# One MoE layer on one core: the shared expert as a group of its own, and one more place for weight tiles

## The reference, cut to what matters

```python
scores = sigmoid(t @ router_w)                    # 64 experts, 8 chosen for each token
gate   = normalised scores of the chosen 8 * 2.5
routed = sum over experts e of (silu(t @ w_gate[e]) * (t @ w_up[e]) * gate[:, e]) @ w_down[e]
shared = (silu(t @ ws_gate) * (t @ ws_up)) @ ws_down
out    = x + g2 * (routed + shared)
```

## Time and profile before

| | us |
|---|---|
| median of 3 runs | 643.5 (642.98 to 643.97) |
| the profiled execution | 645.71 |
| its span, first to last instruction | 643.9 |

### The profile page before, as it was taken

The page is one execution under the profiler, slowest core; times in us unless marked ns, Lnnn a source line. Parts: engine busy times, 40 slices in busy tenths (PEclk is TensorE's granted clock), DMA queues, the critical chain, the costliest instruction groups (busy, mean ns, idle before and its releaser), DMA issues.

```text
span 643.9 us, 11140 instructions
## 1 busy us (share of the span) xinstructions
PE 581.9 (90%) x4568; PEld 406.1 (63%) x4568; DVE 209.9 (33%) x474; ACT 168.2 (26%) x309; POOL 33.6 (5%) x79
## 2 busy tenths in 40 slices
PE   0789999999999999989999999596999999998685
PEld 0478777688877575756675757363567666675352
DVE  0297867787822222111212222020121212121103
ACT  3164727572622121111121212010212121212111
POOL 1240210011100000000000000000000000000002
PEclk9989999999999999999999999898999999999889
DMA  8999599989988999999999999999999999999994
GB/s 329 387 344 389 211 364 383 411 312 397 420 348 365 396 423 415 422 419 421 421 420 420 420 421 419 421 422 421 420 420 421 421 421 421 421 419 420 421 386 155
DMA packets 50662, 252.55 MB, mean 392 GB/s; under 512 B 5912, under 2 KB 11680, under 8 KB 26288
## 3 DMA queue, kind: packets, MB, share of 16 engines
q1 hardware_dynamic: 48240, 246.37, 94.4%
q0 software_dynamic: 1840, 4.21, 2.0%
q10 hardware_dynamic: 528, 1.21, 0.5%
HBM read 250.06 MB, written 1.72 MB: 391 GB/s over the span
## 4 chain that ended last, share of the span: by engine, by line
PE 66%; DMA 19%; SPq 6%; ACT 4%; DVE 2%; issue 1%; POOL 0%; POOLq 0%; DVEq 0%; ACTq 0%
PE bank L1278 21%; PE bank L1354 12%; DMA ring<-in_w_up 8%; PE bank L1249 6%; PE bank L1295 6%; DMA ring<-in_w_down 6%; SPq L556 4%; PE bank L848 3%; DMA ring<-in_w_mod 2%; SPq L627 2%; PE bank L890 2%; PE bank L898 2%; PE bank L894 2%; DMA ccol<-in_c 2%; DMA ring<-in_w_in 1%; PE bank L1011 1%
## 5 line engine op out<-in xcount | busy, mean ns | idle before, releaser
L1278 PE MATMUL bank<-ring,xe 128*64 128x256 f32 (+1 forms) x1520 | 176.1, 397 | 10.7 <-DMA ring<-in_w_up 9.0
L1278 PEld LDWEIGHTS bank<-ring,xe 128*64 128x64 f32 (+1 forms) x1520 | 110.8, 131 | 49.7 <-issue 23.7
L1354 PE MATMUL bank<-ring,actT 128*64 128x512 f32 (+1 forms) x384 | 85.5, 615 | 4.8 <-DMA ring<-in_w_down 3.2
L2325 DVE TENSOR_TENSOR act_e<-bank,sil 128x256 f32<-128x256 f32 x26 | 11.0, 425 | 190.1 <-ACT sil L1741 190.1
L1754 ACT ACTIVATE yhi<-bank,gslot 128x512 fp32r<-128x512 f32 x50 | 34.4, 688 | 113.2 <-PE bank L1354 113.2
L2339 DVE SCALAR_TENSOR_TENSOR ylo<-bank,gslot,yhi 128x512 fp32r<-128x512 f32 x50 | 37.5, 750 | 80.7 <-ACT yhi L1754 80.7
L1741 ACT ACTIVATE sil<-bank 128x256 f32<-128x256 f32 x26 | 10.0, 385 | 194.2 <-PE bank L1278 194.2
L1249 PE MATMUL bank<-pone,hhi 128*128 128x256 f32 x200 | 50.6, 291 | 0.0
L1249 PE MATMUL bank<-pone,hlo 128*128 128x256 f32 x200 | 49.6, 285 | 0.0
L1354 PEld LDWEIGHTS bank<-ring,actT 128*64 128x64 f32 (+1 forms) x384 | 25.2, 130 | 34.9 <-issue 34.7
L1278 PE MATMUL bank<-rows_tile,xe 128*64 128x256 f32 (+1 forms) x128 | 33.5, 422 | 11.1 <-DMA ring<-in_w_up 6.3
(11 more groups left out here) (382 smaller groups left out, 847.5 us busy)
## 6 DMA issues: line engine op xcount, KB each, us to landing
ring<-in_w_gate SPq DMA_DIRECT2D x49, 1024.0 KB, 25.6
ring<-in_w_down SPq DMA_DIRECT2D x48, 1024.0 KB, 26.3
ring<-in_w_up SPq DMA_DIRECT2D x46, 1024.0 KB, 26.4
ring<-in_w_mod SPq DMA_DIRECT2D x12, 2048.0 KB, 13.8
ring<-in_w_in SPq DMA_DIRECT2D x5, 2048.0 KB, 15.7
gb<-in_w_up SPq DMA_DIRECT2D x5, 1024.0 KB, 24.9
spare<-in_w_gate SPq DMA_DIRECT2D x4, 1024.0 KB, 26.9
ring<-in_w_out SPq DMA_DIRECT2D x2, 2048.0 KB, 18.8
```

The lines of the kernel that those rows point to most:

```text
L1278: ins = mm(bank[6][j * w:(j + 1) * w, part * FE:(part + 1) * FE], xe[:, k, slots], weights[:, k, :], start=(k == 0), stop=(k == KD - 1))
L1354: ins = mm(bank[4 + h][j * w:(j + 1) * w, :], actT[:, f, j * w:(j + 1) * w], weights[:, f, 512 * h:512 * h + 512], start=(f == 0), stop=(f ...
```

## The change

The tokens of the shared expert are no longer read from `hT`. Group 7 (`SHARED`) is followed by one more gather, group 8, of all 256 tokens: `pone` is filled with a full one-hot pattern (`every_token`), and `xe` then holds all tokens in transposed form. The shared gate and up products read `xe`. Both are now made in one place, in group 7 behind the second step's `activations_turned`; then the gather of the next routed group follows, and `shared_down`. The numbers of all later gathers go up by one. `sg0` and the half product in group 2 are gone. `ws_gate` and `ws_up` are read in the layout `(p k) f`, whose rows are 8 KB long. The memory of `hT` becomes a place for tiles, `OVER_HT`: tile 16 is loaded there once `hb1_1` is made, and each later tile replaces the one used 17 before it.

```diff
-STEPS, GROUPS = 6 + 10 * TURNS, 3 + 5 * TURNS
+STEPS, GROUPS = 6 + 10 * TURNS, 4 + 5 * TURNS
+SHARED = 5 * (TURNS - 1) + 2
-FILL = [0, 1, OVER_Y, 2, 3, 4, 5, 6, 7, 8, 9, 10, OVER_XN, SPARE, OVER_GB, 11]
+FILL = [0, 1, OVER_Y, 2, 3, 4, 5, 6, 7, 8, 9, 10, OVER_XN, SPARE, OVER_GB, 11, OVER_HT]
-        plan += banks("sg0:4 pos:1 counts:5")
+        plan += banks("pos:1 counts:5")
...
-            sp.dma_start(ws[:, 0:EW].rearrange("p (k f) -> p k f", k=KD),
-                         t["ws_gate"][0].rearrange("(k p) f -> p k f", k=KD)).then_inc(wsg_loaded, 16)
+            sp.dma_start(ws[:, 0:EW], t["ws_gate"][0].rearrange("(p k) f -> p (k f)", k=KD)).then_inc(ws_loaded, 16)
...
+            product(sp, "hb1_1")
+            load_first(NTILE + 4)
...
-                        ins = mm(ps[:, j * 256:(j + 1) * 256], w[:, k, j::JF], hT[:, k, :], start=(k == 0), stop=(k == KD - 1))
+                        ins = mm(ps[:, j * 256:(j + 1) * 256], w[:, k, j::JF], xe[:, k, :], start=(k == 0), stop=(k == KD - 1))
-            pe.wait_ge(wsg_loaded, 16)
-            complete("sg0", shared_product(claim("sg0"), 0, (0,)))
+            def shared_gate_up(group):
+                pe.wait_ge(x_copied, group * 4 + 4)
+                pe.wait_ge(ws_loaded, 48)
+                shared_product(bank[7], 0).then_inc(sg_filled, 1)
+                shared_product(bank[4], EW).then_inc(su_filled, 1)
...
-                if shared == "gate":
-                    shared_gate()
-                elif shared == "rest":
-                    shared_up()
                 gate_up(kind, 1, n + 1, unit, group, again, spread=ends)
...
-                if not last:
+                if shared:
+                    for q in range(4):
+                        gather(q, group + 1)
+                elif not last:
                     gather(0, group + 1)
                 activations_turned(n + 1)
+                if shared:
+                    shared_gate_up(group + 1)
+                    pe.wait_ge(sg_copied, 1)
+                    gather(0, group + 2)
+                    pe.wait_ge(sact_ready, 1)
...
                     for q in range(1, 4):
-                        gather(q, group + 1)
-                if shared == "rest":
+                        gather(q, next_group(group))
+                if shared:
                     shared_down()
...
                 if par == 1 and not last:
                     gathered(group + 1)
+                if shared:
+                    shared_gate()
+                    gathered(group + 2)
...
+                    if shared:
+                        dve.wait_ge(x_filled, (SHARED + 1) * 4 + 4)
+                        one_hots(following, e + 2 * kind, posm_s)
+                        shared_act()
                     turned(following, 0, n_pair + 1)
```

More of the change, by code:

```diff
@@ L66 @@
 FIRST_STEP = [sum(1 if v in QUAD_UNITS else 2 for v in range(u)) for u in range(UNITS)]
-SPARE, OVER_GB, OVER_XN, OVER_Y, OVER_ROWS = NTILE, NTILE + 1, NTILE + 2, NTILE + 3, NTILE + 4
-FILL = [0, 1, OVER_Y, 2, 3, 4, 5, 6, 7, 8, 9, 10, OVER_XN, SPARE, OVER_GB, 11]
+SPARE, OVER_GB, OVER_XN, OVER_Y, OVER_ROWS, OVER_HT = (NTILE + i for i in range(6))
+FILL = [0, 1, OVER_Y, 2, 3, 4, 5, 6, 7, 8, 9, 10, OVER_XN, SPARE, OVER_GB, 11, OVER_HT]
 ROWS_FREE = len(FILL) + 4
@@ L368, in build @@
         out_done = sem("out_done")
-        tile_loaded = [sem(f"tile_loaded{i}") for i in range(NTILE + 5)]
+        tile_loaded = [sem(f"tile_loaded{i}") for i in range(NTILE + 6)]
         last_columns = [sem(f"last_columns{i}") for i in range(2)]
@@ L1161, in _, with shared_product @@
             turn_back(1)
-            def shared_product(ps, off, parts=range(JF)):
+            def shared_product(ps, off):
                 w = ws[:, off:off + EW].rearrange("p (k f) -> p k f", k=KD)
-                for j in parts:
+                for j in range(JF):
                     for k in range(KD):
-                        ins = mm(ps[:, j * 256:(j + 1) * 256], w[:, k, j::JF], hT[:, k, :], start=(k == 0), stop=(k == KD - 1))
+                        ins = mm(ps[:, j * 256:(j + 1) * 256], w[:, k, j::JF], xe[:, k, :], start=(k == 0), stop=(k == KD - 1))
                 return ins
-            pe.wait_ge(wsg_loaded, 16)
-            complete("sg0", shared_product(claim("sg0"), 0, (0,)))
             pe.wait_ge(chosen_ready, 1)
@@ L1222, in gather_first @@
                 evacuated(pe, "x2T3")
-                evacuated(pe, "sg0")
+                evacuated(pe, "rt0")
                 pe.wait_ge(first_stream, 1)
@@ L1237, in gather_first, with next_group @@
                             ins.then_inc(x_filled, 1)
+            def next_group(group):
+                return group + (2 if isinstance(group, int) and group == SHARED else 1)
             def gather(q, group):
@@ L1347, in down @@
                         if par == 1 and not last:
-                            pe.wait_ge(x_copied, group * 4 + 7)
+                            pe.wait_ge(x_copied, next_group(group) * 4 + 3)
                     elif par == 0:
@@ L1380, in sort_slots, with two_steps @@
                 ins.then_inc(sorted_filled, 1)
-            def two_steps(kind, e, n, group, unit, following, gates=gate_s, before=True, starts=False, shared=None, ends=False,
+            def two_steps(kind, e, n, group, unit, following, gates=gate_s, before=True, starts=False, shared=False, ends=False,
                           again=False):
@@ L1438, in first_round @@
                 for it in range(TURNS):
-                    two_steps(QUAD, 24 * it + 8, 10 * it + 4, 5 * it + 2, 6 * it + 2, PAIR, shared=("gate", "rest")[it])
+                    group = 5 * it + 2
+                    two_steps(QUAD, 24 * it + 8, 10 * it + 4, group, 6 * it + 2, PAIR, shared=(group == SHARED))
                     for i in range(4):
-                        two_steps(PAIR, 24 * it + 16 + 4 * i, 10 * it + 6 + 2 * i, 5 * it + 3 + i, 6 * it + 4 + i,
+                        two_steps(PAIR, 24 * it + 16 + 4 * i, 10 * it + 6 + 2 * i, next_group(group) + i, 6 * it + 4 + i,
                                   PAIR if i < 3 else QUAD)
@@ L1719, in _ @@
             A(table_load[:, :], rstd[:, 1, 0:1], ACT.Silu)
-            ps = product(act, "sg0")
-            drain("sg0", A(ssil[:, 0, :], ps[:, 0:NST * P], ACT.Silu))
             def gathered_first():
@@ L1737, in gathered, with pair @@
                       ACT.Copy).then_inc(x_copied, 1)
-            def pair(par, n_pair, group, last=False, starts=False, ends=False, more=0):
+            def pair(par, n_pair, group, last=False, starts=False, shared=False, ends=False, more=0):
                 act.wait_ge(e_filled, n_pair + 1)
@@ L1758, in shared_gate @@
                 act.wait_ge(sg_filled, 1)
-                A(ssil[:, 1, :], bank[7][:, NST * P:2 * NST * P], ACT.Silu).then_inc(sg_copied, 1)
+                A(ssil[:, :, :].rearrange("p a b -> p (a b)"), bank[7][:, :], ACT.Silu).then_inc(sg_copied, 1)
             def keep_g2(n, first):
@@ L1773, in two_steps @@
                     keep_g2(0, NST)
-                pair(1, n + 1, group, last, ends=ends, more=more)
+                pair(1, n + 1, group, last, shared=shared, ends=ends, more=more)
             def first_round():
@@ L1779, in first_round @@
                 two_steps(2, 1)
-                two_steps(4, 2, shared=True)
-                with act.Fori(3, GROUPS - 1) as it:
+                with act.Fori(2, SHARED) as it:
                     two_steps(it * 2, it)
+                two_steps(SHARED * 2, SHARED, shared=True)
+                with act.Fori(SHARED + 1, GROUPS - 2) as it:
+                    two_steps(it * 2, it + 1)
                 two_steps(STEPS - 2, GROUPS - 1, last=True, ends=True)
@@ L2320, in turned, with pair @@
                 ins.then_inc(t_copied, 1)
-            def pair(kind, par, e, n_pair, following, starts=False, ends=False, more=0):
+            def pair(kind, par, e, n_pair, following, starts=False, shared=False, ends=False, more=0):
                 dve.wait_ge(e_silu, n_pair + 1)
@@ L2343, in pair @@
                         sorted_out()
-                    one_hots(following, e + 2 * kind, posm_s)
+                    if shared:
+                        every_token()
+                    else:
+                        one_hots(following, e + 2 * kind, posm_s)
             def finish_all(par, n_pair):
@@ L2362, in two_steps, with every_token @@
             def two_steps(kind, e, n, following, starts=False, shared=False, ends=False, more=0):
[L2363 to L2366, removed]
+                pair(kind, 0, e, n, following, starts, shared, more=more)
+                pair(kind, 1, e, n + 1, following, shared=shared, ends=ends, more=more)
+            def every_token():
+                for s in range(NST):
+                    ins = V.tensor_scalar(pone[:, s, :, :].rearrange("p a b -> p (a b)"), iota[:, :], gate[:, s, 0:1, 1], None,
+                                          ALU.is_equal)
```

(5 more changed lines are left out.)

19 lines of the change are left out of this document (4 added, 15 removed).

## The result

The changed kernel took 645.64 us (median of 7, 644.53 to 646.49), the kernel before 643.38 (7 runs): a ratio of 1.0035, 95% interval 1.002 to 1.005. A second set, of an unchanged copy, gave 1.0043 (1.0028 to 1.0059). The change makes the kernel slower by 2.3 us. The forecast was 643.9 us, no change, with a range up to 646.7 and 0.38 on slower. The time lies in the range, but not where the forecast put it. Single executions of one kernel spread more than the 0.15% given ahead of the forecast: 28 of the kernel before lie between 641.65 and 644.85 us, 0.5% apart. Only medians of many show a difference of this size.

What follows compares the result with a forecast made beforehand. DMA tile stream and TensorE were taken as nearly in balance. Terms: -2.49 (place) + 1.0 (start) + 18.8 (added work) - 16.9 (group 12 waits and half clock) = +0.4 us; 643.9 us at the median, range 641.6 to 646.7.

Steps and rivals of the forecast that it cites:

- The place: Tile 16 loads near 169.7 us without waiting for the gate pass; whole stream one tile early, -2.49 us (bounds 0 and -2.49).
- The first gap closed: Sign of being right: the stream's first stop, near 184 us, is filled by tile 16's earlier load.
- The start: Ahead of the first gather: without sg0 TensorE idles and its clock falls earlier, +1.0 us (bounds 0 and +2.0).
- Group 7: Up pass stays 5.29 us; behind it second gather, copy wait, shared gate and up add 18.8 us; group 8 starts at 482.5.
- The stop of the stream: Near 484 us, down tiles of group 7 freed late: 0.5 to 1 us lost, bounds 0 and 3.
- a DMA gap over 2 us at 484: Sign of being wrong: the tile stream stops for over 2 us around group 7's late down tiles.
- a low clock for more than 3 us behind 441: Sign of being wrong: TensorE's clock stays low around the start of group 7's second up pass, forecast at 441.5.
- Group 12: Tiles ready, clock 1.00: TensorE 17.3 us late at its start, 0.4 at its end; TensorE decides by 1 us.
- The sum: Whole kernel: +0.4 us on the profiled execution, span 644.3; carried to the median, 643.9 us, no change.
- A: Rival, slower: clock falls in group 7 ahead of gate and up passes, start at its bound; +3.0, 646.5 us; chance 0.31.
- B: Rival, faster: clock holds at the start and in the up pass, the stream decides; 641.8 us; chance 0.17.
- C: Rival: the place's gain is lost again at 484 us, so it is 0; +2.9, 646.4 us; chance 0.07.

Runs made afterwards that it cites:

- no_place: The changed kernel without its 18th place for tiles, so 16 places in turn and not 17: 649.3 us, ratio 1.0112 to the kernel before.
- warm: The changed kernel with 16 unused products of ident and ones where sg0 stood: 643.72 us, ratio 1.0011 to the kernel before.
- at_six: The changed kernel with the shared expert's work behind group 6, ahead of the second QUAD group: 644.62 us, ratio 1.0025 to the kernel before.
- at_two: The changed kernel with the shared expert's work in group 2, the first QUAD group, not group 7: 643.98 us, ratio 1.0012 to the kernel before.
- no_shared: The changed kernel without the shared expert's gather, gate, up and down products, its weights still read: 642.91 us, ratio 0.9996 to the kernel before.
- before_late_sg: The kernel before with only sg0 moved from ahead of the first gather into group 2: 644.87 us, ratio 1.0025 to the kernel before.
- down_first: The changed kernel with shared_down moved behind the second down products of group 7: 647.09 us, ratio 1.0055 to the kernel before.
- before_again: The kernel before, unedited, with a second profile: ratio 1.0012, profiled execution 642.88 us.
- two_warm: The changed kernel with the edits of at_two and warm together: 641.76 us, ratio 0.9988 to the kernel before.
- two_warm_down: two_warm with shared_down behind the second down products of group 2: 642.3 us, ratio 0.9983 to the kernel before; run again, 641.28 us, 0.9968.

## Why the prediction was right or wrong

**The place: right in kind.** Tiles come earlier by it, and no_place shows that it is needed. "The first gap closed" was wrong: the gap moved. Between 180 and 190 us the stream lost 2.8 us in the first profile of before and 2.3 in the changed one, whose first release came 1.1 us later; the rest may lie in the faster ws loads, which no run separates. In warm, with the clock at 1.00, the gap is closed.

**The start: the term that was mis-sized.** I took +1.0 us on top of a profile in which the clock had already fallen, and met that profile's start nearly: +1.1 us (182.38 against 181.26). Some of this was luck, since in the changed profile TensorE reached the router 0.6 us earlier. Against the other execution of before, in which the clock did not fall here, the start is 3.0 us later, and 1.3 us in the change's second profile. Eight profiles of kernels without sg0 or its stand-in (the change twice, no_place, at_six, at_two, no_shared, before_late_sg, down_first) have a mean clock of 0.50 to 0.66 from 173 to 177 us. Of six with sg0 or the 16 products five have 1.00 (before_again, warm, two_warm, two_warm_down twice), and the sixth, the first of before, 0.96 with the fall behind it. How often the clock falls in the kernel before is not known; one profile of two. before_late_sg gives the mean cost, 1.6 us, or 0.6 more than my term.

**Group 7: the added work right, its surroundings not.** Second gather 3.86 us (3.83 forecast), wait for its last copy 0.67 (0.65) on the chain, products 14.09 (14.2), start of group 8 481.3 (482.5, of which 0.6 is an earlier arrival at the router). The up pass took 5.35 us (5.29) in one profile and 6.32, near the upper bound, in the other. The stop of the stream was 2.6 us in one and 3.6 in the other, where I took 0.5 to 1 with a bound of 3. Two of the forecast's own signs of being wrong, a DMA gap over 2 us at 484 and a low clock for more than 3 us behind 441, are there: the gap in both profiles, the low clock barely in the first (441 to 444) and to 444.5 in the second, where it had begun at 438.

**Group 12: right but for what comes last.** No tile wait up to the column pieces, clock 1.00. Down products at 613.1, the second piece at 632.06. TensorE was to decide by 1 us; it waited for the piece, 0.35 and 0.63 us.

**The sum: right for the profile, wrong for the median.** For the profiled execution I forecast a span of 644.3; it was 643.6, and 643.2 in the second. That the time fell into the range is owed to the range's width: "no change" was the forecast, and the change is slower beyond its interval. The step that failed is "The runs shown have a median 2.2 below the profiled one, 643.5; the difference carries over". It didn't, since a good part of these 2.2 us was the low clock at the start, which this change makes the rule. By the second profile of before my own steps give: -2.5 (place), +3.0 (start), so the last up tile of group 7 at +0.5 (measured +0.4), +18.8 and -16.9 behind it: +2.4, where the chain's end moved by +2.2 and the medians by +2.3. With the change's second profile they give -2.5 + 1.3, so that tile at -1.2 (measured -1.1), and +0.7 at the end; there the slower up pass adds 1.1, which makes +1.8, and the end moved by +2.0. So the 2.3 us are what the start and the clock in group 7 leave together, in shares that differ from one execution to the next.

**The rivals.** A had the sign and nearly the time (646.5), though its sum adds 0.6 and 0.8 where its own words give 1.0 and 1.0. Its mechanism is there in part. The clock fell under the up pass of group 7 as it says: in one profile of the change at no more cost than before, in the other at +1.0 us, and in warm at +1.2. The start, which it took near its upper bound, did the rest. B needed a clock that holds; none of the eight profiles of kernels that make no products there has one at the start. C fell with no_place.

## What to carry to other kernels

Before the median is used as the base of a sum, compare the profiled execution with it: if they differ by more than the effect in question, look for the stretch in which that execution was unusual, and ask whether the change turns this into the rule. Work that is hidden beside another engine is not free to remove: here 3.6 us of it kept TensorE's clock up for the dense stretch behind, and useless products in its place bought back 1.5 us. And 19 us of work put behind the last tile wait of group 7 used up all the waits that were left, 16.8 us, and cost the rest. The same work ahead of more tile waits costs less: two_warm_down is 0.2 to 0.3% under before, where the place alone would be worth 0.4% by the forecast's one tile. For that the places of the next tiles have to be freed in time, and so the products that free them go first.

## What the runs showed of the hardware

The same 16 products of 128 x 256 took 2.14 us at clock 1.00 and 3.75 at 0.50. The Trainium skill, TensorE: Matmul & The Clock Gate, What's actually happening, says that activity releases the throttle; warm and before_late_sg agree from both sides: 16 products added where TensorE was idle raised the clock from 173 to 177 us from 0.50 to 1.00, and products taken away from there lowered it to 0.50. One execution, that of down_first, had a granted clock of 0.95 outside the stretches at the low level. Its gate and up passes took 7.20 us where the change's took 6.91, and the whole was 7.6 us longer than the median of the kernel's other runs (646.72). None of the other profiles has this level, and its cause is open.
